# Sums over partitions with one or two moving columns, each stationary operand taken as four strips of 32 columns

## The reference, cut to what matters

```
ada  = silu(c) @ w_ada + b_ada                    # shift, scale and gate columns of the first layer
h2   = rmsnorm(x, norm_ffn) * (1 + sc2) + sh2
x    = x + g2 * conv_ffn(h2)                      # ends with u @ w_down
x    = rmsnorm(x, norm_final)                     # mean of x*x over the width
h    = rmsnorm_2(x, g_mix)                        # second layer: mean of x*x once more, after the gain
q    = rmsnorm_2(q, q_gain)                       # 8 heads of 64, in forgetting_attention
```

## Time and profile before

| | |
|---|---|
| time, median of 3 runs | 972.4 us (971.21 to 973.9) |
| span of the profiled execution, first to last instruction | 964.8 us |
| busy: PE, PEld, DVE, ACT | 936.9, 882.2, 740.8, 476.6 us |
| instructions in the profile | 17895 |
| mean TensorE clock granted | 0.996 |
| bytes moved | 171.77 MB, 178 GB/s in the mean |

### The profile page before, as it was taken

One profiled execution on the slowest core, in us unless ns is written; L12 is line 12 of the kernel. 1 busy time (PEld: TensorE's weight loads), 2 busy tenths in 40 slices (PEclk: granted clock), 3 DMA queues, 4 the chain that ended last, 5 costly groups with the idle time before them and its releaser, 6 DMA issues.

```text
span 964.8 us, 17895 instructions
## 1 busy us (share of the span) xinstructions
PE 936.9 (97%) x7646; PEld 882.2 (91%) x7646; DVE 740.8 (77%) x1098; ACT 476.6 (49%) x571; POOL 14.8 (2%) x34
## 2 busy tenths in 40 slices
PE   5999999999989999999999999999999999999997
PEld 3689999999989999999999899999999999999986
DVE  3689988888898988857956985545686987887863
ACT  3545435636546565438754743324645444334453
POOL 0000000002000000000200000000000000000000
PEclk9999999999999999999999999999999999999999
DMA  9998354465558656424553334333355555555541
GB/s 339 367 292 266 102 174 132 132 218 161 176 164 269 223 188 210 171 88 174 191 205 135 128 116 158 133 132 99 121 177 173 197 178 195 193 177 194 184 146 44
DMA packets 114046, 171.77 MB, mean 178 GB/s; under 512 B 3240, under 2 KB 96704, under 8 KB 109872
## 3 DMA queue, kind: packets, MB, share of 16 engines
q1 hardware_dynamic: 111680, 165.63, 51.3%
q0 software_dynamic: 1088, 2.57, 0.9%
q10 hardware_dynamic: 1200, 2.43, 0.7%
HBM read 169.55 MB, written 1.06 MB: 177 GB/s over the span
## 4 chain that ended last, share of the span: by engine, by line
PE 64%; DVE 8%; ACT 4%; issue 2%; DMA 1%; DVEq 0%; ACTq 0%
PE bank L1167 20%; PE bank L1168 19%; PE bank L1169 19%; DVE wlo L626 3%; PE bank L1734 2%; ACT whi L617 2%; DVE arena L2284 1%; ACT arena L977 1%; DVE arena L2370 1%; DMA raw<-in_w_up_dram 1%; DVE arena L1961 0%; PE bank L1206 0%; PE bank L1201 0%; ACT arena L847 0%; DVE XT L2236 0%
## 5 line engine op out<-in xcount | busy, mean ns | idle before, releaser
L1167 PE MATMUL bank<-hhi,whi 128*128 128x256 f32 (+1 forms) x1744 | 506.8, 291 | 6.7 <-ACT whi L617 1.9
L1168 PE MATMUL bank<-hlo,whi 128*128 128x256 f32 (+1 forms) x1744 | 500.2, 287 | 0.0
L1169 PE MATMUL bank<-hhi,wlo 128*128 128x256 f32 (+1 forms) x1744 | 500.1, 287 | 0.0
L626 DVE TENSOR_TENSOR wlo<-raw,whi 128x2048 fp32r<-128x2048 f32 x131 | 299.5, 2288 | 110.7 <-ACT whi L617 87.4
L1167 PEld LDWEIGHTS bank<-hhi,whi 128*128 128x128 f32 x1744 | 334.1, 192 | 16.1 <-issue 9.9
L1168 PEld LDWEIGHTS bank<-hlo,whi 128*128 128x128 f32 x1744 | 334.3, 192 | 4.0 <-issue 1.2
L1169 PEld LDWEIGHTS bank<-hhi,wlo 128*128 128x128 f32 x1744 | 334.2, 192 | 2.5
L617 ACT ACTIVATE whi<-raw 128x2048 fp32r<-128x2048 f32 x131 | 250.1, 1913 | 141.1 <-PE bank L1169 127.0
L1167 PE MATMUL bank<-whi,hhi 128*128 128x256 f32 (+1 forms) x256 | 87.5, 342 | 0.8 <-ACT arena L1127 0.8
L1168 PE MATMUL bank<-wlo,hhi 128*128 128x256 f32 (+1 forms) x256 | 86.4, 337 | 0.0
L1169 PE MATMUL bank<-whi,hlo 128*128 128x256 f32 (+1 forms) x256 | 86.2, 337 | 0.0
(11 more groups left out here) (362 smaller groups left out, 828.9 us busy)
## 6 DMA issues: line engine op xcount, KB each, us to landing
raw<-in_w_up_dram SPq DMA_DIRECT2D x44, 1024.0 KB, 5.1
raw<-in_w_in_tiles_dram SPq DMA_DIRECT2D x32, 1024.0 KB, 4.9
raw<-in_w_down_dram SPq DMA_DIRECT2D x22, 1024.0 KB, 4.9
raw<-in_w_ada_dram SPq DMA_DIRECT2D x19, 1024.0 KB, 5.5
raw<-in_w_in_dram SPq DMA_DIRECT2D x14, 1024.0 KB, 5.6
raw<-in_w_branch_dram SPq DMA_DIRECT2D x6, 1024.0 KB, 5.1
arena<-in_w_ada_dram SPq DMA_DIRECT2D x10, 512.0 KB, 9.9
raw<-in_w_out_dram SPq DMA_DIRECT2D x4, 1024.0 KB, 5.0
```

Source lines behind the costliest of these rows:

```text
L626: dve.tensor_tensor(wlo[:, g % RING, :], raw[:, n % RING, :], whi[:, g % RING, :].bitcast(F32), ALU.subtract).then_inc(w_lo, 1)
L1167: pe.matmul(o, wh, ah, start=start, stop=False, **kw)
L1168: pe.matmul(o, wh, al, start=False, stop=False, **kw)
L1169: return pe.matmul(o, wl, ah, start=False, stop=stop, **kw)
```

## The change

A helper `strip_sums` is added. It takes what one of these sums was given, and issues four matmuls in its place: one for each 32 columns of the stationary operand, each writing the 32 output partitions that belong to them. The moving operand, the numbers computed and the order of the places in PE's list stay the same. All seven blocks of sums (units A2 to A5, the `both_sums`, `rq`) use it. The setting-up sums near the start (`row_turn`, line 1229) are left as they were.

```
--- before.py
+++ after.py
@@ -308,6 +308,7 @@
         std, rstd = slot(16, 1, 0, 512), slot(16, 1, 512, 512)
         S = [slot(8, 1, 512 * n, 512).rearrange("p (h t) -> p h t", h=HEADS) for n in range(2)]
         HALVES = (slice(0, 64), slice(64, P))
+        STRIPS = [slice(32 * n, 32 * n + 32) for n in range(4)]
         MV = slot(4).rearrange("p (a v) -> p a v", a=2)
         S_WIDE = slot(8).rearrange("p (m t) -> p m t", m=8)
         S_Q = slot(15, 1, 512, 512).rearrange("p (m t) -> p m t", m=8)
@@ -1269,6 +1270,14 @@
             row_turn(7)
             keep_clock(bank[7], 5)
 
+            def strip_sums(o, at, stationary, moving, start, stop):
+
+                n = moving.shape[1]
+                for r in STRIPS:
+                    ins = pe.matmul(o[r, at:at + n], stationary[:, r], moving, start=start, stop=stop,
+                                    skip_group_check=True)
+                return ins
+
             def ada_unit(a):
 
                 o = g_open(f"A{a}")
@@ -1276,9 +1285,7 @@
                 for c in range(4 * a, 4 * a + 4):
                     for nb in range(2):
                         at = 2 * (c % 4) + nb
-                        src = XC[:, c % 8, :]
-                        ins = pe.matmul(o[:, at:at + 1], src[:, P * nb:P * (nb + 1)], ones[:, 0:1],
-                                        start=True, stop=True)
+                        ins = strip_sums(o, at, XC[:, c % 8, P * nb:P * (nb + 1)], ones[:, 0:1], True, True)
                 ins.then_inc(g_full, 1)
 
             def gemm(name, w, g0=None, n_tok=T, units="unit", part=(0, 1), lo=0):
@@ -1490,8 +1497,8 @@
                 pe.wait_ge(sq_ready, 4 + g + 1)
                 for k in (2 * g, 2 * g + 1):
                     for t in range(2):
-                        ins = pe.matmul(o[:, 2 * t:2 * t + 2], SQ[:, T * k + P * t:T * k + P * (t + 1)], weigh[:, k, :],
-                                        start=k == 0 and t == 0, stop=k == KT - 1, skip_group_check=True)
+                        ins = strip_sums(o, 2 * t, SQ[:, T * k + P * t:T * k + P * (t + 1)], weigh[:, k, :],
+                                         k == 0 and t == 0, k == KT - 1)
                 return ins
 
             def down(j, tag="f"):
@@ -1532,8 +1539,8 @@
                     pe.wait_ge(ada_late, 16)
                     for c in range(4):
                         for nb in range(2):
-                            ins = pe.matmul(o[:, 2 * c + nb:2 * c + nb + 1], acc_late[:, c, P * nb:P * (nb + 1)],
-                                            ones[:, 0:1], start=True, stop=True)
+                            ins = strip_sums(o, 2 * c + nb, acc_late[:, c, P * nb:P * (nb + 1)], ones[:, 0:1], True,
+                                             True)
                     ins.then_inc(m_full, 1)
             down(FFT // 2 - 2)
             m_open("sum2")
@@ -1600,8 +1607,7 @@
             o = m_open("rq")
             for a in range(2):
                 for c in range(4):
-                    ins = pe.matmul(o[:, 8 * a + 2 * c:8 * a + 2 * c + 2], fq_sq[:, c, P * a:P * (a + 1)],
-                                    half[:, 0:P:64], start=True, stop=True)
+                    ins = strip_sums(o, 8 * a + 2 * c, fq_sq[:, c, P * a:P * (a + 1)], half[:, 0:P:64], True, True)
             ins.then_inc(m_full, 1)
             gemm("scc1", T)
             gemm("scv0", T)
```

## The result

The changed kernel takes 963.82 us (median of 5 executions, 961.24 to 966.34), the kernel before 972.4 (5 executions, 971.17 to 973.9): a ratio of 0.9929, 95% interval 0.9912 to 0.9947, so 5 to 9 us less (6.9 by the ratio, 8.6 by the two medians of five). The profiled execution of the change has a span of 962.0 us and a device time of its own, 963.82, which is 1.8 us more than its span.

What follows compares the result with a forecast made beforehand. PE was taken as the bound, busy for 97% of the span, with weight loads pacing the sums. 1.15 + 0.96 + 1.12 + 0.96 = 4.2 us off 964.8, plus 7.6, gave 968.2 us; range 965.6 to 973.8.

Steps and rivals of the forecast that it cites:

- The sum of 4.2 us: Gains of A4, A5, `both_sums` and `rq` added up, taken off the profiled span of 964.8 us to give 960.6.
- The pace of a pass: In all blocks of sums: four strip loads side by side, 8 ns a pass, a sum 64 ns for 224.
- The rivals of 16 and 28 ns: Two strips at a time, 970.5 us, chance 0.13; a pace four groups cannot beat, 973.8 us, chance 0.15.
- the one that went by the Trainium skill: Overhead of about 60 cycles, about 25 ns, for each matmul, paid four times a sum; near 973 us, no separate chance.
- Entering and leaving: Costs around a block of strips: 0.21 us ahead, 0.15 behind; a block of 8 between products 1.06 us for 2.02.
- A2 and A3 at nothing: Worth 0 each: PE already waits for DVE behind them, at `level(1)` and `wo2`, and would only wait longer.
- A4 1.15, A5 0.96, both_sums 1.12, `rq` 0.96: Gains in us: ahead of `sum1`, between products, at the end of `down`, and between products ahead of the scores.
- The slower rival: Strip loads wait for one another, 56 ns a pass; 984 us; chance 0.04.
- the hidden one: Gain of A5 or `rq` ends in a wait that has no row yet; 3.2 us less gain, 969.2 us; chance 0.05.
- the 7.6 us that the median of the runs stands above it: Added to the forecast span of 960.6 us to reach the forecast time of 968.2 us.
- the clock: Rival behind `both_sums(3)`: PE's clock stays up, `sum3` starts 1.4 us sooner, 966.8 us; chance 0.15.

Runs made afterwards that it cites:

- e8_strip_by_strip: Changed kernel with A2 to A5 and `rq` doing all sums of one 32-column strip before the next; 969.1 us, 0.9997 of the kernel before.
- e7_halves: Changed kernel with each operand taken in two parts of 64 columns instead of four strips; 965.65 us, 0.9965 of the kernel before.
- e13_whole_fill2: Kernel before, sums whole, with two clock-keeping matmuls added in PE's wait ahead of `both_sums(3)`; 968.81 us, 0.9969 of the kernel before.
- e3_only_a2_a3: Strips at A2 and A3 alone, all other sums whole as in the kernel before; 971.34 us, 1.0012 of the kernel before.
- e1_base: The kernel before, run once more without an edit; 970.14 us, ratio 0.9992.
- e6_strips_keep3: Changed kernel with three instead of five clock-keeping matmuls between `both_sums(3)` and `sum3`; 962.36 us, 0.9924 of the kernel before.

## Why the prediction was wrong

The sum of 4.2 us was right, step by step, and what it was subtracted from was not.

- *The pace of a pass* was forecast at 8 ns and measured at 8. The law behind it, a strip's load a quarter as long and four side by side, agrees with `e8_strip_by_strip` (27 ns alone) and `e7_halves` (28 ns). The rivals of 16 and 28 ns fall with it. So does the one that went by the Trainium skill, "TensorEngine Tiling (Array Packing)", Instruction Overhead: by its 60 cycles each, which I estimated at 25 ns a matmul, the time would have come out near no change (973). The trace doesn't agree: 64 passes of one moving column start 8 ns apart in the mean. Within one column group, at 27 ns, it would have agreed.
- *Entering and leaving* as priced: A5 1.07 us for 1.06, A4 to `sum1` 0.64 for 0.65.
- *A2 and A3 at nothing*: right as far as the runs tell (1.0012, 0.9994 to 1.0030). Between `level(0)` and `level(1)` are 3.4 to 3.7 us with and without strips at A2. `wo2` starts 21.46 us behind `z0` before and after; its wait grew to 1.1 where I said 1.4, so that 0.3 of A3's gain was lost at other places, most of it 14 to 15 us behind `z0`.
- *A4 1.15, A5 0.96, both_sums 1.12, `rq` 0.96*: measured 1.16, 0.95, 1.20 and 0.95, in all 4.26. Against the profiled execution from which the sum was made, the change took 786.1 - 781.8 = 4.2 us off the way from `z0` to the end.
- *The slower rival and the hidden one* are out by the same numbers.

**The first step that failed** is in the way from the sum to the time: "the 7.6 us that the median of the runs stands above it". The profile and the median were not of one execution. In the runs here, of every kernel, the device time is 1.7 to 2.1 us above the span of the same execution (3.1 in a single one), mostly 1.8. The 129 executions of the kernel before that are counted here have a mean span of 968.65 us (964.5 to 972.5), so its time is 970.4 in the mean. The profiled execution, at 964.8, was among its fastest, and the first median, 972.4, was 2.0 us above that mean, within the spread of single executions. I could have suspected it: nothing in the trace explains 7.6 us outside the program.

**The second is the clock**, which the sum left out, or rather left to a rival with a chance of 0.15: 1.4 us if it stayed up, and "at most half of 3.4 us" for one more fall. With whole sums, five of seven traces (all with the five clock-keeping matmuls and no filled wait) have 6.8 us at the lower clock around `both_sums(3)`, and only two, the first profile among them, have 3.4. With strips there, all six have 3.4 (the halves, in their one trace, 6.8). Each further 3.4 us costs 1.65 us: 210.58, 208.93 and 207.33 us from `fg0` to `dq0` with whole sums and two, one or none, and 206.77 and 205.1 with strips and one or none. (The 205.1 also has three clock-keeping matmuls for five.) So in these traces the strips go with one low stretch where the whole sums mostly have two. My rival named the right place, but the clock did not stay up: it fell in all six, and against the first profile, from which the sum was made, nothing was saved. The profiled execution had itself escaped the second stretch; that was its luck, and part of why it was fast. That a low stretch costs this time whatever the length of the sums is shown by `e13_whole_fill2`, where whole sums without a low stretch are 3.3 us faster with more work in the list. From `z0` to the end the usual whole kernel takes 787.75 us and that with strips 781.85: 5.9 less. The 17 executions of the changed kernel have a mean span of 962.5 us, 6.1 less than the 129, with an uncertainty of about 0.8 (95%) from their spread.

By these numbers, known only afterwards, 970.4 - 4.2 - 1.7 = 964.5 would have been the forecast if every execution of the kernel before had the second low stretch, and 965.0 with five in seven; 1.8 + 962.5 = 964.3 is the mean measured. The two terms together bring it below the range's 965.6; either alone would not have.

**What stays open.** Whether the low stretch behind A4, 1.68 us in `e3_only_a2_a3` and `e8_strip_by_strip` (2 of 10 traces in which A4 took its long time, none of 8 in which it was shorter), belongs to the gain in the mean: too few traces. What decides, in the kernel with whole sums, between one low stretch and two is not settled either. In the traces with two, the lower level begins within 0.5 us of `both_sums(3)`'s first sum (425.6 and 425.61 in `e1_base`); in the two others it begins 1.5 and 1.1 us behind it (425.3 and 423.84 in the first profile). Nor do I know whether `e6_strips_keep3` had no low stretch because of its edit or by chance. And the start of `z0` differs by up to 6 us between traces (178.69 to 184.70), with a low stretch near 17 us in many, ahead of all the sums changed.

A2 too lies ahead of `z0`, and so outside the stretches above. There is a low stretch at `level(1)`, right behind A2: 3.4 us in the first profile, but 6.8 us in the three later traces of the kernel before, as the windows of `e1_base` show:

```profile
101.30:104.70 3.40, 2.72 (x37) 2.52 (x37) 3.40 (x4) 1.03 (x2) 0.00 (x0) 0.51 0.02 5
104.70:108.10 3.40, 3.40 (x18) 3.40 (x18) 3.30 (x7) 1.29 (x2) 0.00 (x0) 0.50 0.81 251
```

From `level(1)` to `z0` are 78.3 to 78.4 us with 6.8 us of it (4 of 10 traces with whole sums at A2, none of 8 with strips or halves there) and 77.3 to 77.6 otherwise. So a part of the gain in the mean, up to 0.8 us, may come from A2 by way of the clock; `e3_only_a2_a3` shows no such gain in its time, and it stays open.

## What to carry to other kernels

Where only one or two columns moved, the load of the stationary operand set the pace, and four strips of 32 columns in turn over the four column groups made a two-pass sum cost 64 ns instead of 224; the strips of one operand must stand next to each other in the list. Make a sum against the mean of many executions and not against one profile: look whether time minus span fits, and whether the profiled execution has the usual number of low-clock stretches. A wait between thin matmuls right ahead of a critical step is worth filling with wide ones, as a trial: here it paid 1.5 to 4.6 us (the interval of `e13_whole_fill2`).

## What the runs showed of the hardware

- Four column groups in turn take 64 loads of 32 columns in 0.63 us, 8 ns each, while one group alone takes them at 27 ns and two groups of 64 columns at 28.
- The same program, with the same waits ahead of it (0.94 us), is granted the lower clock around `both_sums(3)` for 3.4 us in one execution and for 6.8 in another, and the further 3.4 us cost 1.65, about half.
- Adding two matmuls in a wait of 0.94 us left no low stretch there in the one trace taken (3.3 us less in the stage than with two of them), and the whole kernel was faster by about 3 us (0.9969, 0.9953 to 0.9985).
